# Window queries turned in 32x32 squares by VectorE and moved through DRAM, heads one slot later

## The reference, cut to what matters

```
q = partial_rope_2(q_in.reshape(B, S, SW_Q_HEADS, SW_HEAD_DIM), positions)
k = partial_rope_2(k_in.reshape(B, S, SW_KV_HEADS, SW_HEAD_DIM), positions)
scores = jnp.einsum('bnqhgd,bnkhd->bnhgqk', qb, kw) * (SW_HEAD_DIM ** -0.5)
scores = jnp.where(mask, scores, -jnp.inf)
m = jnp.maximum(jnp.max(scores, axis=-1, keepdims=True), sink)
p = jnp.exp(scores - m)
probs = p / (jnp.sum(p, axis=-1, keepdims=True) + jnp.exp(sink - m))
o = jnp.einsum('bnhgqk,bnkhd->bnqhgd', probs.astype(vw.dtype), vw)
```

## Time and profile before

| | us |
|---|---|
| median of 3 runs | 1694.58 (1694.19 to 1695.52) |
| the profiled execution's own time | 1694.39 |
| its span, first to last instruction | 1692.6 |
| PE busy in the span | 1667.4 (99%) |
| DVE / ACT / POOL busy | 1164.5 / 959.9 / 228.4 |
| DMA queue of SP | 49.3% of 16 engines |

### The profile page before, as it was taken

How to read it: one execution, slowest core, us unless ns; L and a number is a source line. 1 busy time by engine, 2 the same in 40 slices (tenths; PEclk the granted TensorE clock), 3 DMA queues, 4 the chain that set the end, 5 groups by cost and what they waited for, 6 DMA issues and landing times.

```text
span 1692.6 us, 29404 instructions
## 1 busy us (share of the span) xinstructions
PE 1667.4 (99%) x11401; PEld 1363.7 (81%) x11401; DVE 1164.5 (69%) x2144; ACT 959.9 (57%) x1818; POOL 228.4 (13%) x318
## 2 busy tenths in 40 slices
PE   9999999999999999999999999999999999999998
PEld 7887888888778788876787788888876787788887
DVE  6757667766676676688867666566678877676665
ACT  5458475444775744587644465446577644554553
POOL 2203000022120000432302000000432302000000
PEclk9999999999999999999999999999999999999999
DMA  8754744567456455633323556554633323446552
GB/s 312 262 197 148 253 140 163 178 207 267 170 177 223 148 176 164 224 123 103 125 96 106 174 168 206 185 184 138 221 120 125 102 99 126 163 161 207 180 179 82
DMA packets 142884, 286.94 MB, mean 170 GB/s; under 512 B 6175, under 2 KB 9371, under 8 KB 141723
## 3 DMA queue, kind: packets, MB, share of 16 engines
q1 hardware_dynamic: 140688, 282.22, 49.3%
q10 hardware_dynamic: 2059, 2.85, 0.5%
HBM read 275.61 MB, written 9.44 MB: 168 GB/s over the span
## 4 chain that ended last, share of the span: by engine, by line
PE 85%; ACT 5%; DVE 4%; POOL 3%; issue 2%; DMA 0%; DVEq 0%; POOLq 0%; ACTq 0%; SPq 0%
PE bank L444 21%; PE bank L446 20%; PE bank L445 20%; PE bank L425 5%; PE bank L427 3%; PE bank L478 2%; PE bank L436 1%; PE bank L434 1%; PE bank L435 1%; ACT scratch L2026 1%; ACT hi L397 1%; DVE lo L407 1%; PE bank L1814 1%; DVE buf L2178 1%; PE bank L675 1%
## 5 line engine op out<-in xcount | busy, mean ns | idle before, releaser
L444 PE MATMUL bank<-hi,xhl 128*128 128x512 f32 (+1 forms) x1728 | 697.0, 403 | 3.6 <-DVE lo L407 2.1
L446 PE MATMUL bank<-hi,xhl 128*128 128x512 f32 (+1 forms) x1728 | 672.9, 389 | 0.0
L445 PE MATMUL bank<-lo,xhl 128*128 128x512 f32 (+1 forms) x1728 | 670.8, 388 | 0.0
L407 DVE TENSOR_TENSOR lo<-raw,hi 128x1024 fp32r<-128x1024 f32 (+1 forms) x504 | 612.7, 1237 | 54.3 <-PE bank L446 39.2
L397 ACT ACTIVATE hi<-raw 128x1024 fp32r<-128x1024 f32 (+1 forms) x504 | 519.4, 1050 | 201.1 <-PE bank L446 169.0
L444 PEld LDWEIGHTS bank<-hi,xhl 128*128 128x128 f32 x1728 | 324.7, 188 | 81.1 <-issue 15.6
L446 PEld LDWEIGHTS bank<-hi,xhl 128*128 128x128 f32 x1728 | 324.3, 188 | 70.2
L445 PEld LDWEIGHTS bank<-lo,xhl 128*128 128x128 f32 x1728 | 325.4, 188 | 57.9
L425 PE MATMUL bank<-xhl,hi 128*128 128x512 f32 x384 | 136.0, 398 | 0.0
L427 PE MATMUL bank<-xhl,lo 128*128 128x256 f32 x384 | 107.8, 281 | 0.0
L425 PEld LDWEIGHTS bank<-xhl,hi 128*128 128x128 f32 x384 | 72.2, 188 | 17.8
(11 more groups left out here) (323 smaller groups left out, 1944.4 us busy)
## 6 DMA issues: line engine op xcount, KB each, us to landing
raw<-in_w_in SPq DMA_DIRECT2D x135, 1024.0 KB, 5.1
raw<-in_w_ff SPq DMA_DIRECT2D x64, 1024.0 KB, 5.2
raw<-in_w_proj_a SPq DMA_DIRECT2D x8, 1024.0 KB, 5.0
raw<-in_w_proj_b SPq DMA_DIRECT2D x8, 1024.0 KB, 5.0
raw<-in_w_out SPq DMA_DIRECT2D x8, 1024.0 KB, 5.3
raw<-in_w_up_sw SPq DMA_DIRECT2D x8, 1024.0 KB, 5.0
raw<-in_w_up_dn SPq DMA_DIRECT2D x8, 1024.0 KB, 5.1
raw<-in_w_o SPq DMA_DIRECT2D x8, 1024.0 KB, 5.1
```

The lines of the kernel that those rows point to most:

```text
L407: dve.tensor_tensor(self.lo[g % LO_RING][:, 0:w], src, self.hi[g % HI_RING][:, 0:w].bitcast(F32), ALU.subtract).then_inc(self.lo_ready, 1)
L444: pe.matmul(out, xh[:, row, t], self.hi[slot % HI_RING][:, w], start=first, stop=False)
L445: pe.matmul(out, xh[:, row, t], self.lo[slot % LO_RING][:, w], start=False, stop=False)
L446: mm = pe.matmul(out, xl[:, row, t], self.hi[slot % HI_RING][:, w], start=False, stop=last)
```

## The change

The four steps that turned the window queries on TensorE and the four copies of ScalarE are gone. In their place, in each of the two layers:

- POOL rotates the queries ahead of the keys.
- In slot 3 of dk VectorE transposes both token blocks in 32x32 squares into `ys` (step `flip`), and SP writes the result to DRAM in four DMAs.
- In slot 5 of dk SP waits for these and reads the 1 MB back into `qs` (step `flip_in`).
- The scores of a pair of heads are made in 16 products with 32 stationary columns each, where it was 4 products with 128.
- The keys are turned in slot 6 of dk, which was slot 4, and each `work[t]` stands one slot later: `work[0]` was in the last slot of dk and now is in the first of dq. So the even lists, which hold a pair of scores, now share their slots with the turns of dk and dq; before, the odd ones did.
- SP's program, which was only loads in block two, now walks the list of steps as the other engines do, and issues a load at most so far ahead of the current piece (`load_ahead`).

```diff
@@ plan_two
     work = turned_values("s", HEADS)
-    p.run(sec("dk", D), [[("rope", "sk", 0), ("rope", "sk", 1), ("rope", "sq", 0)], [("rope", "sq", 1)], [], [],
-                         [("turn", "sk", 0)], [], turns("sq")[0] + turns("sq")[1], turns("sq")[2] + turns("sq")[3] + work[0]])
+    p.run(sec("dk", D), [[("rope", "sq", 0), ("rope", "sq", 1), ("rope", "sk", 0)], [("rope", "sk", 1)], [], [("flip", "sq")],
+                         [], [("flip_in", "sq")], [("turn", "sk", 0)], []])
...
-    p.run(sec("dq", 0), [b + a + c for a, b, c in zip(conv("dk"), work[1:9], keys)])
+    p.run(sec("dq", 0), [b + a + c for a, b, c in zip(conv("dk"), work[0:8], keys)])
...
-    p.run(sec("dv", 2 * D), [a + d + b + c for a, b, c, d in zip(work[9:17], conv("dq"), norms, sums)])
-
-    slots = delta_slots(work[17:])
+    p.run(sec("dv", 2 * D), [a + d + b + c for a, b, c, d in zip(work[8:16], conv("dq"), norms, sums)])
+
+    slots = delta_slots(work[16:])
@@ block_two, tensor
                 if kind == "s_scores" and arg % 2 == 0:
...
-                    pe.wait_ge(*at("sq_copied", arg // 4))
                     if arg == 0:
+                        pe.wait_ge(*at("flipped", "sq"))
                         pe.wait_ge(*at("turn_copied", ("sk", 0)))
...
-                    for b, r in zip(SCORE, rows):
-                        pe.matmul(B[b][:, 0:P], qT_(qs)[r, arg // 2, 0:P], ks[r, k, 0:P], start=True, stop=True)
...
+                    for i in range(4):
+                        for b, r in zip(SCORE, rows):
+                            pe.matmul(B[b][strip(i), 0:P], queries(arg // 2, 0, i, r), ks[r, k, 0:P], start=True, stop=True)
+                    for i in range(4):
+                        for b, r, h in zip(SCORE, rows, (arg, arg + 1)):
+                            mm = pe.matmul(B[b][strip(i), P:3 * P], queries(arg // 2, 1, i, r), ks[r, k, :], start=True, stop=True)
@@ block_two, vector
+                if kind == "flip":
+
+                    dve.wait_ge(*at("rotated", "sq"))
+                    for tb in range(TB):
+                        y = ys[:, :, :].rearrange("p a b -> p (a b)").rearrange("p (j f t a) -> p t j f a", j=4, f=KB, t=TB)[:, tb]
+                        ins_ = dve.transpose(y, b0[:, tb, :].rearrange("p (f j a) -> p j f a", f=KB, j=4))
+                    ins_.then_inc(*up("flip_turned", "sq"))
@@ block_two, sync
-        for u in range(core.units_issued, len(core.units)):
-            core.load_unit(sp, u)
+        for plan in plans:
+            for what in plan.all_steps(s):
+                kind, arg = what[0], what[1] if len(what) > 1 else None
+                if kind in ("piece", "first"):
+                    core.load_ahead(sp, plan.base + arg)
+                if kind == "flip":
+                    y = ys[:, :, :].rearrange("p a b -> p (a b)").rearrange("p (j x) -> p j x", j=4)
+                    sp.wait_ge(*at("flip_turned", "sq"))
+                    for i in range(4):
+                        sp.dma_start(flip_room(plan.layer)[:, :, i, :].rearrange("j a x -> a j x"),
+                                     y[strip(i), :, :]).then_inc(*up("flip_out", ("sq", i), 16))
+                if kind == "flip_in":
+                    sp.wait_ge(*at("flip_out", ("sq", 3)))
+                    sp.dma_start(qs[:, :, :].rearrange("p a b -> p (a b)"),
+                                 flip_room(plan.layer)[:, :, :, :].rearrange("j a i x -> (j a) (i x)"))\
+                      .then_inc(*up("flipped", "sq", 16))
```

More of the change, by code:

```diff
@@ L1530, in block_two, with flip_room, queries @@
     silu_tanh = [scr[:, 3072 + 512 * i:3584 + 512 * i].rearrange("p (n t) -> p n t", n=2) for i in range(2)]
+    def flip_room(layer):
+        if layer not in rooms:
+            rooms[layer] = nc.dram_tensor(f"flip_sq{layer}", (4, QUARTER, 4, 4 * P), F32, kind="Internal").ap()
+        return rooms[layer]
+    def queries(f, tb, i, r):
+        return qs[r, :, :].rearrange("p a b -> p (a b)").rearrange("p (i f t b) -> p f t i b", i=4, f=KB, t=TB)[:, f, tb, i]
     def ended(plan, name):
@@ L1935, in _ @@
                                        scale=half_of[arg]).then_inc(*up("high", (arg, f, 1)))
-                if kind == "turn" and arg == "sq":
-                    f = what[2]
-                    act.wait_ge(*at("turned", (arg, f)))
-                    act.activation(qT_(qs)[:, 2 * f:2 * f + 2, :],
-                                   B[core.turn_bank[s.stage, arg, f]][:, :].rearrange("p (j t) -> p j t", j=2), ACT.Copy)\
-                       .then_inc(*up("sq_copied", f))
                 if kind == "tanh":
@@ L1983, in _ @@
                     c = int(arg[2])
[L1984 removed]
+                    dst, before = {"dk": (b1, None), "dq": (b0, at("flip_turned", "sq") if arg == "dq0" else None),
+                                   "dv": (b1, at("turned", ("dk", 3)) if arg == "dv0" else None)}[arg[:2]]
                     if c == 0 and before:
[L1986 removed]
+                        act.wait_ge(*before)
                     if arg == "dk0":
```

20 lines of the change are left out of this document (9 added, 11 removed).

## The result

The changed kernel takes 1716.06 us (median of 4 runs, 1715.31 to 1717.36) against 1694.51 for the kernel before: 1.0128 times as long, 95% interval 1.0116 to 1.0140, or 21.5 us more. The prediction said 1709.5, with 1699 to 1719 as its range. The profiled execution took 1717.36 us, with a span of 1715.6, 23.0 more than before. Lines of the changed kernel are numbered up to 16 higher than before: the scores are L1713 and L1716, the convolution L2192 and L2194, the turn of the probabilities L1726, the betas L1758, the last cut L2351.

The account below looks back on a forecast made before the run. TensorE, busy 99% of the span, was taken to bound the kernel. Per layer -1.6 + 5.0 + 4.4 + 0.4 + 1.9 - 2.55 = +7.55 us, two layers +15.1 on 1694.4: 1709.5 us, range 1699 to 1719.

Parts of the forecast that it names:

- sign: Whole kernel: slower by more than 0.2% with chance 0.86, within 0.06, faster 0.08.
- The strips: Scores of a head pair: 16 strips cost as much as 4 products, within 0.1 us a pair.
- the turns: Sixteen query transposes removed from TensorE in each layer: 1.6 us less a layer.
- The flip: Ahead of the first scores, TensorE waits 5.0 us a layer for the transposed queries, bounds 1.4 and 9.1.
- The convolution: Jobs dq1, dv0, dv1, gb0 wait for VectorE's convolution 0.8, 1.2, 1.2, 1.2: 4.4 us a layer.
- The turns of heads: Slot 2 of dq: turn of head 0 waits 0.4 us for its reciprocal, bounds 0 and 1.
- betas: In gb, betas of pair 1 waits 1.9 us for the last cut to free bank OUT, bounds 0 and 2.5.
- What goes: Old TensorE waits at L1681, L1725, L444 and L478 disappear: together 2.55 us a layer.
- the clock: Rival: after the flip's 5 us idle TensorE comes back slow, +0.9 us a layer, 1711.3 us; chance 0.20.
- Quick transfers: Rival: the flip through DRAM costs 1.4 us of waiting instead of 5.0, time 1702.3 us; chance 0.14.
- The harmless shift: Rival: VectorE runs ahead, so waits of 4.4, 0.4 and 1.9 don't come, time 1696.1 us; chance 0.12.
- the faster case: Rival: queries arrive before TensorE at 721.5 and VectorE keeps up, -4.15 us a layer, 1686.1 us; chance 0.08.

Follow-up runs that it names:

- best2: Changed kernel with flip one slot earlier, heads' lists one slot later still, and betas of pair 1 in a scores bank instead of OUT: 1691.78 us.
- sinks ahead: Changed kernel with GpSimd writing the sinks of head h+1 in the slot of head h, nothing else: 1713.08 us.
- TensorE kept at work: Changed kernel with 24 added 128x128 products that nobody reads ahead of the wait for the flip: 1714.80 us.
- early flip: Changed kernel with the flip in slot 2 of dk and its read in slot 3, instead of 3 and 5: 1708.11 us.
- the last experiments: Changed kernel with earlier flip, later heads' lists, betas in another bank: 1691.78 us; the same with sinks one head ahead and squares of dk one slot later: 1690.11.
- sink_ahead: Kernel before with the heads' lists one slot later and GpSimd writing the sinks one head ahead: 1701.18 us.

## Why the prediction was right in its sign, and 6.4 us short

**The strips** came out, and **the turns** as far as the time of best2 shows it. A stretch with an output product, a turn and a pair takes 2.13 us before and 2.09 with strips, from its first product to the stream's next (first two rows: the kernel before; last two: the run best2, where the strips stand in the same company):

```profile
734.87 0.65 PE L1725 MATMUL bank<-scratch,buf 128*64 128x256 f32 x4
...
737.00 0.50 PE L444 MATMUL bank<-hi,xhl 128*128 128x512 f32 x1
...
739.18 0.65 PE L1737 MATMUL bank<-scratch,buf 128*64 128x256 f32 x4
...
741.27 0.50 PE L444 MATMUL bank<-hi,xhl 128*128 128x512 f32 x1
```

**The flip.** Chain, forecast against trace: transposes end 710.6 and 710.9; writes issued 712.3 and 712.5; read issued 720.5 and 721.56, the writes having landed in up to 7.2 us and not 6.3; read 6.0 and 5.0; landing 726.5 and 726.6; wait 5.0 and 5.4. Each link is right within 1.1 us. That the landing came out within 0.1 us is luck: the writes took 0.9 us longer and the read 1.0 less than I had them.

**The convolution.** 0.8, 1.2, 1.2, 1.2 forecast; 0.8, 1.5, 2.3, 0.6 measured, 5.3 for 4.4. The mis-sized piece is the "0.1 to start" of VectorE: at dv1 it started late behind the chain sinks, exponential, reciprocal, which I hadn't followed over GpSimd. With the sinks ahead dv1 waits 1.5, dv0 still 1.5, and the sum is 4.5. The 0.3 at each of dv0 and dv1 that remains is a wait of the cut for ScalarE's high part (0.31 at 756.5), and at gb0 I had 0.6 too much.

**The turns of heads** 1.0 more for 0.4; **betas** 1.6 for 1.9. **What goes**: 3.7 for 2.55, since L1681 lost all of its wait of 1.75 and not 0.9, and L1691, which my sum left out, half of its 0.6. Together these waits net 9.6 a layer in the trace, and the forecast's terms, without the turns, 9.15.

**The step that failed** is that the sum has no term for the clock. It stood among the rivals, with a chance of 0.20 and at one place only, behind the flip, at 0.9 a layer net. At that place it is confirmed: the fall is there in both layers and goes when TensorE is kept at work. Its price was about right, 0.65 net by a difference at the edge of the noise. The measured time is nearer to this rival's 1711.3 than to the forecast. What I did not see is the second place. I had written 1.2 us for the waits ahead of dv0 and dv1 and asked of none of them what they would do to the clock; one came out at 2.3, and the clock fell behind it, in both layers. In the trace the two falls take 3.65 us a layer, and with the 0.45 of the waits that is the whole miss of 4.1 a layer in that execution. By medians the miss is 6.4 us (21.5 for 15.1). Two runs took something away from the changed kernel, each by itself: 3.0 (sinks ahead) and 1.3 (TensorE kept at work). They were never made together, and the rest, some 2 us if they add up, was not isolated.

The row on which I had rested the rival's price, the program's start with a granted clock that reads full while products ran at half rate, is of no use for this: there the column did not follow the rate. In the flip's wait it did fall, to 0.50, together with the rate (a product every 0.43 us for 0.23).

The Trainium skill, TensorE: Matmul & The Clock Gate, part 1, says in "HAM oscillation" that waits for data between stretches of products make the array lose its clock; the trace agrees, with 0.50 behind a wait for data of 5.4 us. That a wait of 2.3 can do it, and at another place not, is what the traces here show.

**The other rivals.** Quick transfers did not happen: from the issue of the first write to the issue of the read it took 9.1 us, and the read 5.0; with the early flip 6.9 and 6.4. The price that spoke for this rival, a fixed 2.0 us and the bytes at 436 GB/s, is given by the Trainium skill, DMA: Bandwidth & Descriptors, "Anatomy of one DMA — SWDGE (gpsimd) path", as a fit of DMAs that GpSimd issues; here SP issues them, so it was no close neighbour. The harmless shift did not happen either: the shift alone cost 13.2 us; the faster case neither, though the last experiments reach it, by lists one slot later and not by a read 5 us earlier alone.

## What to carry to other kernels

Moving a list of steps by one slot is a change of its own: look at what it newly stands beside, and follow the chain over every engine that serves a step there, the lightly loaded ones too, before calling a wait 1.2 us. Price a wait of the matrix engine twice, once for its length and once for the clock that may fall behind it, and for the second part look at the granted clock in stretches of a few microseconds, not on the page. A transfer that must land by a time wants no load issued just ahead of it; a wait that can't be shortened can be met later, if what is moved keeps its parity with its neighbours.

## What the runs showed of the hardware

- Four writes of 256 KB from the core's memory to DRAM land in 2.7 to 5.3 us when the last load was issued 7 us before, and in 6.2 to 7.2 right behind a load of 1 MB on the same queue; a read of 1 MB took 5.0 us with the last load 6.7 us ahead and 6.3 to 6.5 with one 3 to 4 us ahead. The Trainium skill, DMA: Bandwidth & Descriptors, "Queues, rings and completion order", has each DMA engine consume one ring's descriptors in order; the trace fits that, since the writes lose 2 to 3.5 us behind the load.
- An operation of GpSimd's rotation that takes 0.45 us by itself took 3.64 or 4.77 when it started beside three or four splits of VectorE in a row, and ended 0.3 us behind the last of them. The Trainium skill, SBUF — State Buffer, "Who interferes with whom", calls the ports that the two share an exclusive lock and not a division of bandwidth; the trace agrees, with the numbers above. In the changed kernel this is 4.3 us of the flip's chain, as an estimate from these two times.
- The granted clock fell to half behind the waits of 5.1 to 5.9 us for the flip and of 3.8 for the square of dq, in both layers each time. Behind waits of 2.2, 2.3 and 3.0 it fell in some places and stayed full in others of the same length. Behind those of 1.5 in sink_ahead it stayed full. No bound is read from this.
- A product of 128x128 in this number format (f32) takes 0.225 us at the upper clock and stands in the trace as two entries of 0.11: 44 took 9.9 us.
